# Expert weights of a mixture-of-experts encoder: gate and up loads cut in half along the contraction, down loads of the third pair moved up

## What is computed

```python
for g in range(N_GROUPS):
    a = jnp.einsum('td,edf->tef', t, w_gate[g])      # d = 1024, f = 256
    u = jnp.einsum('td,edf->tef', t, w_up[g])
    act = jax.nn.silu(a) * u * combine[:, g, :, None]
    y = y + jnp.einsum('tef,efd->td', act, w_down[g])
```

## Time and profile before

| | |
|---|---|
| time of the profiled execution | 859.02 us |
| its span | 857.3 us |
| median of three runs | 860.95 us |
| PE busy | 781.7 us (91% of the span) |
| DVE, ACT, POOL busy | 378.9, 282.9, 143.8 us |
| gate and up products (L1869) | 226.3 us busy, 25% of the chain that ended last |
| down products (L1895) | 122.4 us busy, 14% of the chain |
| moved by DMA | 245.52 MB, 286 GB/s over the span |

### The profile page before, as it was taken

How to read it: one execution, slowest core, us unless ns; L and a number is a source line. 1 busy time by engine, 2 the same in 40 slices (tenths; PEclk the granted TensorE clock), 3 DMA queues, 4 the chain that set the end, 5 groups by cost and what they waited for, 6 DMA issues and landing times.

```text
span 857.3 us, 11051 instructions
## 1 busy us (share of the span) xinstructions
PE 781.7 (91%) x4303; PEld 426.8 (50%) x4303; DVE 378.9 (44%) x701; ACT 282.9 (33%) x522; POOL 143.8 (17%) x135
## 2 busy tenths in 40 slices
PE   3877889999999999899999878998999999989897
PEld 3656835534434333346888655455343434434355
DVE  6998543622122221217858678426212222121164
ACT  5251143522121221216755445324212122121163
POOL 6695500200000000000066563001000000000000
PEclk9988989999999999999999889999999999999999
DMA  6052195399999999996579550352699999999931
GB/s 222 1 156 100 23 425 232 119 373 420 420 421 421 421 421 421 421 404 234 196 177 314 223 169 1 159 234 99 277 421 421 420 421 421 421 420 422 410 126 49
DMA packets 55493, 245.52 MB, mean 286 GB/s; under 512 B 14002, under 2 KB 15088, under 8 KB 30480
## 3 DMA queue, kind: packets, MB, share of 16 engines
q1 hardware_dynamic: 53344, 240.34, 70.1%
q0 software_dynamic: 2096, 4.45, 2.6%
HBM read 243.17 MB, written 1.60 MB: 286 GB/s over the span
## 4 chain that ended last, share of the span: by engine, by line
PE 80%; DVE 8%; POOL 4%; issue 4%; ACT 2%; DMA 1%; SPq 0%; DVEq 0%; ACTq 0%
PE PS L1869 25%; PE PS L1895 14%; PE PS L1646 11%; PE PS L1909 7%; PE PS L1805 3%; PE PS L2143 3%; PE PS L2118 2%; PE PS L1760 2%; PE PS L1820 2%; PE PS L2097 2%; PE PS L2029 2%; POOL s5V L608 2%; PE PS L1739 1%; POOL qrs L677 1%; PE PS L1878 1%
## 5 line engine op out<-in xcount | busy, mean ns | idle before, releaser
L1869 PE MATMUL PS<-ring,xw 128*64 128x512 f32 x1024 | 226.3, 593 | 14.1 <-issue 12.5
L1869 PEld LDWEIGHTS PS<-ring,xw 128*64 128x64 f32 x1024 | 77.3, 137 | 155.8 <-issue 155.7
L1895 PE MATMUL PS<-ring,actT 128*64 128x512 f32 x512 | 122.4, 603 | 1.4 <-DVE actT L1373 1.4
L572 POOL TENSOR_TENSOR rstd<-ms,mhalf 128x2 f32<-128x2 f32 x6 | 4.3, 710 | 583.6 <-DVE ms L1037 578.2
L1373 DVE COPY actT<-PS 128x256 f32<-128x256 f32 x32 | 13.6, 424 | 179.6 <-PE PS L1878 172.0
L886 ACT ACTIVATE ohi<-PS 128x512 fp32r<-128x512 f32 x64 | 38.2, 598 | 160.6 <-PE PS L1895 160.6
L1062 DVE SCALAR_TENSOR_TENSOR ringr<-ring,gcol,dwh 128x512 fp32r<-128x512 f32 x80 | 62.8, 835 | 26.9 <-ACT dwh L737 26.9
L1387 DVE TENSOR_TENSOR olo<-PS,ohi 128x512 fp32r<-128x512 f32 x64 | 44.1, 689 | 63.8 <-ACT ohi L886 62.3
L878 ACT ACTIVATE act<-PS,wslot 128x256 f32<-128x256 f32 x32 | 15.2, 474 | 171.7 <-PE PS L1869 171.7
L737 ACT ACTIVATE dwh<-ring,gcol 128x512 fp32r<-128x512 f32 x80 | 52.8, 716 | 34.2 <-PE PS L1646 34.2
L1646 PE MATMUL PS<-ringr,hTh 128*128 128x512 f32 x160 | 63.2, 395 | 0.0
(11 more groups left out here) (332 smaller groups left out, 1060.8 us busy)
## 6 DMA issues: line engine op xcount, KB each, us to landing
ring<-in_moe_w_gate SPq DMA_DIRECT2D x64, 1024.0 KB
ring<-in_moe_w_up SPq DMA_DIRECT2D x64, 1024.0 KB
ring<-in_moe_w_down SPq DMA_DIRECT2D x64, 1024.0 KB, 25.6
ring<-in_nat_w_qkv SPq DMA_DIRECT2D x6, 2048.0 KB
ring<-in_ple_w_gate SPq DMA_DIRECT2D x4, 2048.0 KB
ring<-in_s_w_out SPq DMA_DIRECT2D x2, 2048.0 KB
ring<-in_nat_w_o SPq DMA_DIRECT2D x2, 2048.0 KB
ring<-in_s_w_in SPq DMA_DIRECT2D x1, 2048.0 KB
```

Source lines behind the costliest of these rows:

```text
L1869: ins = mm(PS[CAP * h_:CAP * h_ + CAP, 0, :].rearrange("p (u f) -> p u f", u=2), xw[:, p % 2, k, CAP * h_:CAP * h_ + CAP], wv[h_][:, k], s ...
L1895: ins = mm(PS[CAP * h_:CAP * h_ + CAP, 2 + n, :], actT[:, k, CAP * h_:CAP * h_ + CAP], wd[h_][:, k, 512 * n:512 * n + 512], start=k == 0, ...
```

## The change

`load_gate_up` becomes two functions. `load_early` asks for floats 0 to 1023 of gate and of up (k = 0 to 3 of the contraction), after a new signal `gu_half`, which the last product of k = 3 of pair p - 3 gives. `load_late` asks for the other halves after `gu_done` as before. Each of the four loads of an expert is 0.5 MiB, 4 KB in one piece per partition. PE waits for the early halves at the start of `gate_up` and for the late ones ahead of k = 4, by a semaphore of their own for each two slots. The down loads of pair 2 are asked for right behind its gate and up loads, ahead of those of pair 3. To stay within the number of semaphores, some others are merged: the down loads of two slots share one; in the setup of the first layer `rp_loaded` and `gcol_loaded` become `vectors_loaded`, `dt_ready` goes into `trig_ready`, and `ldt_wide` into `ang_ready`.

```diff
@@ the waits @@
         loaded = [S(f"slot_loaded{s}") for s in range(6)]
-        down_loaded = [S(f"down_loaded{s}") for s in range(6)]
+        late_loaded = [S(f"late_loaded{s}") for s in range(3)]
+        down_loaded = [S(f"down_loaded{s}") for s in range(3)]
...
+        def late_arrived(eng, n):
+            eng.wait_ge(late_loaded[items[n][0] // 2], 64 * nth_moe[n])
+
         def down_arrived(eng, n):
-            eng.wait_ge(down_loaded[items[n][0]], 16 * nth_moe[n])
+            eng.wait_ge(down_loaded[items[n][0] // 2], 32 * nth_moe[n])
@@ SP @@
-            def load_gate_up(n):
+            def load_early(n):
+
+                s, (gate_, up_, _) = items[n]
+                if prev[n] is not None:
+                    name, value = done[prev[n]]
+                    sp.wait_ge(S("gu_half" if name == "gu_done" else name), value)
+                sp.dma_start(ring[s][:, 0:1024], gate_[1][:, 0:1024]).then_inc(loaded[s], 32)
+                sp.dma_start(ring[s][:, 2048:3072], up_[1][:, 0:1024]).then_inc(loaded[s], 16)
+
+            def load_late(n):
+
                 s, (gate_, up_, _) = items[n]
                 if prev[n] is not None:
                     name, value = done[prev[n]]
                     sp.wait_ge(S(name), value)
-                sp.dma_start(ring[s][:, 0:2048], gate_[1]).then_inc(loaded[s], 32)
-                sp.dma_start(ring[s][:, 2048:4096], up_[1]).then_inc(loaded[s], 16)
+                sp.dma_start(ring[s][:, 1024:2048], gate_[1][:, 1024:2048]).then_inc(late_loaded[s // 2], 16)
+                sp.dma_start(ring[s][:, 3072:4096], up_[1][:, 1024:2048]).then_inc(late_loaded[s // 2], 16)
...
-                        load_gate_up(m0 + 2 * p)
-                        load_gate_up(m0 + 2 * p + 1)
-
-                    if p < 2:
+                        load_early(m0 + 2 * p)
+                        load_early(m0 + 2 * p + 1)
+                        load_late(m0 + 2 * p)
+                        load_late(m0 + 2 * p + 1)
+
+                    if p < 3:
                         load_down(i, 2 * p)
                         load_down(i, 2 * p + 1)
-                    elif p > 2:
+                    elif p > 3:
@@ PE, gate_up and down @@
                 for k in range(k0, k1):
+                    if k == KD // 2:
+                        late_arrived(pe, moe_item[i] + 2 * p)
...
+                    if k == KD // 2 - 1:
+                        ins.then_inc(S("gu_half"), 1)
...
-                    if n == 0:
+                    if n == 0 and h_ == 0:
                         down_arrived(pe, it)
```

More of the change, by code:

```diff
@@ L451, in load_down @@
                     sp.wait_ge(S("d_done"), 2 * (NP * i + (e - 6) // 2) + 2)
-                sp.dma_start(ring[s][:, 4096:6144], down_[1]).then_inc(down_loaded[s], 16)
+                sp.dma_start(ring[s][:, 4096:6144], down_[1]).then_inc(down_loaded[s // 2], 16)
             sp.dma_start(lam[:, 0], I["s5_lam_re"][0].rearrange("d g p -> g d p")).then_inc(S("lam_loaded"), 16)
@@ L630, in _ @@
                 pool.dma_start(gcol[:, BLOCK_GAIN[n], :], gains[n].rearrange("(k p) -> p k", p=P),
-                               allow_slow_non_contiguous=True).then_inc(S("gcol_loaded"), 16)
+                               allow_slow_non_contiguous=True).then_inc(S("vectors_loaded"), 16)
             for n in (1, 4):
                 pool.dma_start(gcol[:, ROW_GAIN[n], :], gains[n].rearrange("(p k) -> p k", p=P))\
-                    .then_inc(S("gcol_loaded"), 16)
+                    .then_inc(S("vectors_loaded"), 16)
             pool.dma_start(rp[:, :, :], I["nat_rpb"][0].rearrange("a b c -> (a b) c")
                            .rearrange("(p a) c -> p a c", a=2))\
-                .then_inc(S("rp_loaded"), 16)
-            pool.wait_ge(S("rp_loaded"), 16)
+                .then_inc(S("vectors_loaded"), 16)
+            pool.wait_ge(S("vectors_loaded"), 16 * 8)
             link(pool.tensor_copy(rpf[:, :, :], rp[:, :, ::-1]))
@@ L641, in _ @@
             pool.wait_ge(S("rpbr_written"), 16)
-            pool.wait_ge(S("gcol_loaded"), 16 * 7)
+            pool.wait_ge(S("vectors_loaded"), 16 * 8)
             router_gain(0)
@@ L750, in _ @@
             ac.activation(dtt[:, :].rearrange("p (b j) -> p b j", j=4), perm(PS[:, 5, 0:SG]), ACT.Exp)\
-                .then_inc(S("dt_ready"), 1)
-            ac.wait_ge(S("ang_ready"), 1)
+                .then_inc(S("trig_ready"), 1)
+            ac.wait_ge(S("ang_ready"), 2)
             ac.activation(pq[:, 6], pq[:, 3], ACT.Sin).then_inc(S("trig_ready"), 1)
@@ L837, in _ @@
                 front(1, n)
-            ac.wait_ge(S("gcol_loaded"), 16 * 7)
+            ac.wait_ge(S("vectors_loaded"), 16 * 8)
             def gather_evict(i, k):
@@ L1073, in _ @@
             ve.wait_ge(S("lam_loaded"), 48)
-            ve.tensor_copy(ldtb[:, :, :], bc(ldt[:, :], 2, SP_)).then_inc(S("ldt_wide"), 1)
+            ve.tensor_copy(ldtb[:, :, :], bc(ldt[:, :], 2, SP_)).then_inc(S("ang_ready"), 1)
             ve.wait_ge(S("prm_T"), 1)
@@ L1079, in _ @@
                                 PS[:, 4, 0:2 * SG].rearrange("p (c j b) -> p c b j", c=2, j=4)))
-            ve.wait_ge(S("dt_ready"), 1)
+            ve.wait_ge(S("trig_ready"), 1)
             link(tt(v[1], im, dtt[:, :], ALU.mult))
@@ L1112, in _ @@
                     .then_inc(S("h_ready"), 1)
-            ve.wait_ge(S("trig_ready"), 3)
+            ve.wait_ge(S("trig_ready"), 4)
             link(tt(v[8], v[5], v[7], ALU.mult))
@@ L1654, in _ @@
                 pe.transpose(PS[:, 4, SG * c:SG * c + SG], lam[:, c].rearrange("g d p -> g (d p)"), ident[0:SG, 0:SG])
-            pe.wait_ge(S("ldt_wide"), 1)
+            pe.wait_ge(S("ang_ready"), 1)
             pe.transpose(PS[:, 5, 0:SG], ldtb[:, :, :].rearrange("g d p -> g (d p)"), ident[0:SG, 0:SG]).then_inc(S("prm_T"), 1)
```

## The result

The changed kernel took 853.43 us (median of six runs, 851.67 to 857.26), the kernel before beside it 861.02 (857.71 to 862.39): a ratio of 0.9924, with an interval of 0.9895 to 0.9954. It is faster, by 7.6 us (the difference of the medians) where the sum had 14.7, and lies above the range of 842.5 to 852.5. The profiled execution took 855.27 us, its span 853.5.

What follows compares the result with a forecast made beforehand. PE waits for weights late in both expert stages; starting the loads earlier wins 7.4 us in layer 0 and 7.3 in layer 1, 14.7 in all, from a mean of 859.7 to 845.0 us, range 842.5 to 852.5.

Steps and rivals of the forecast that it cites:

- the sum: Whole kernel: 7.4 us won in layer 0 and 7.3 in layer 1, 14.7 us in all.
- What bounds the kernel: Expert stages of both layers: PE waits for weights near the end, its lead used up by pair 12.
- the forecast 7.4 and 7.3: Gains in layers 0 and 1: waits of 6.3 and 6.2 us, plus 1.1 each for slower groups.
- The 358.0 for pair 15 without waits: Layer 0: start of pair 15 if PE never waited, in place of 365.31.
- Down loads moved: Pair 2's down loads run in the idle stretch of each layer; the stream behind is 5.0 us shorter.
- The early start: Pair 3 in each layer: `gu_half` comes 4.7 us ahead of `gu_done`, so the stream starts 4.7 us earlier.
- Rate of the shorter pieces: Gate and up loads: 4 KB pieces taken at 421 GB/s; down to 403 PE's work hides the price.
- the 5.8 us to spare: Pair 15, layer 0: late halves come at 355.6 and are needed at 361.4.
- My check of that load: Input of `p_transposes` behind pair 15: PE forward by 7.4 us, stream by 9.7, so it stays covered.
- Added wait, more loads, merges: Wait ahead of k = 4, ten issues for six a pair, merged signals: nothing; the wait at most 6.6 us.
- Everything behind is released by PE's progress and moves along: Work after the expert stages: moves forward with PE, keeping the gains of 7.4 and 7.3 us.
- part of it is lost: Rival: added wait costs up to 0.22 us each, or halves run at 403 to 384 GB/s; 848 to 856, chance 0.14.

Runs made afterwards that it cites:

- e4: The change with halves for pair 3 alone, all other pairs' gate and up in whole loads after `gu_done`, down loads moved: 849.15 us, 0.9881 of the kernel before.
- e5: The change with the early halves too asked for only after `gu_done`, so no early start: 861.04 us, 1.0011 of the kernel before.
- e2: The kernel before with pair 2's down loads moved and the setup's signals merged, gate and up in whole loads after `gu_done`: 854.8 us, ratio 0.9948.

## Why the prediction was wrong

*What bounds the kernel*: right. With weights in time, pairs take 6.87 us and steps 13.1 to 13.4, in both layers, and e4 shows that nearly the whole wait could be won: 6.9 and 6.7 us of the forecast 7.4 and 7.3. (The 358.0 for pair 15 without waits should have been 358.1, which changes nothing.)

*Down loads moved*: right. Alone, they brought pair 15 forward by the 5.0 us forecast, with 2.2 us of waiting left. The stage was shorter by 3.3 only, because the clock fell behind that wait.

*The early start*: the stream did start earlier, and `gu_half` was worth 3.1 to 4.0 us a layer (change against e5). But "its four loads of 0.52 MB last 5.0 us" assumed full rate at once. At 283 GB/s for 174 to 180, the stream falls short of 412 by 6 x 129 = 0.77 MB, 1.9 us.

*Rate of the shorter pieces*: **the step that failed**, together with the full rate at once, just above. The prediction put the price of the pieces at nothing. I took 421 GB/s from two single microseconds of `w_out`. The full stretch runs at 412 with a third of the bytes still in 8 KB pieces: 6.29 MB / 0.412 = 15.27 us a pair, less 4.98 for the down loads, leaves 10.29 us for 4.19 MB, or 408 GB/s. The figure that I had set beside the row, the 408.7 GB/s of the Trainium skill (DMA: Bandwidth & Descriptors, section "iDMA fabric — 4 AXI ports for 8 engines, asymmetric across TPBs"), was the right one; the trace agrees with it. Over 13 pairs it costs 13 x 0.33 = 4.3 us. With the slow start, 6.2 of the 5.8 us to spare are gone: PE waits 0.5 us for pair 15's late halves. And the lead that is left, 9.7 - 4.3 - 1.9 = 3.5 us, is 3.4 short of the 6.9 by which PE is forward after that wait: the load for `p_transposes`, 2.3 us early before, should be 1.1 late, and PE waited 1.7 in layer 0 and 1.1 in layer 1. My check of that load had used the lead without its losses. The rate alone would have left both covered, by 1.5 and 0.3 us; it took the slow start too, for which the prediction had no term. These waits, 2.2 and 1.9 us a layer, are most of the 2.6 and 2.3 that the stages lack to 7.4 and 7.3.

*Added wait, more loads, merges*: nothing, as taken. Groups take 6.87 with the wait in their middle.

*"Everything behind is released by PE's progress and moves along"*: wrong by 2.2 to 2.5 us in the profiled executions. The second mixer, in which the clock falls, took longer behind the changed stage. Its cause is open.

*The sum* for the profiled executions: 4.75 + 4.97 won, 2.5 lost in the middle, and 3.4 lost ahead of the first stage, where the changed kernel's profiled execution was late (167.60) and its second one was not (164.32). Of the 7.1 us that the medians lack to the 14.7, the stages explain 5.0 and the middle about 2. The rival "part of it is lost" came true in its time (848 to 856), but not by either of its conditions: the added wait cost nothing, and the rate was 408, not 403 to 384. That was too strict, because 408 used up what I called spare once the start was slow. I gave that case 0.14.

## What to carry to other kernels

Before cutting loads in pieces, ask where the queue is empty: only there can a load start sooner. Cut those loads and leave the rest whole (e4), and first look for loads that stand behind a wait which isn't theirs, as moving them cost nothing here. A margin that hides a price must be worked out with every loss at once, for each consumer on the way; and a rate is read from a long stretch, not from single microseconds. What is left of a wait can cost more than its length when the clock falls behind it, as in e2. Where TensorE's clock falls between two stages, that stretch may change its length too, so compare stage by stage.

## What the hardware showed

A stream with gate and up in 4 KB pieces and down in 8 KB pieces runs at 412 to 413 GB/s, against 421 with all in 8 KB pieces, whatever the size of a load (0.5 or 1 MiB). That makes 408 for the 4 KB pieces, if the others keep 421.

After a pause such a stream runs at 200 to 350 GB/s in most of its first 7 or 8 microseconds, with the engines' share about 1. With 8 KB pieces it doesn't (e2 has 431 GB/s at 174 to 180). Why is open, and the length of the pieces alone doesn't explain it: the load of `w_out` in the kernel before, 4 KB pieces behind a pause as well, reaches 365 and 422 GB/s within 4 us of its first bytes:

```profile
73.00:74.00 1.00, 0.00 (x0) 0.00 (x0) 0.97 (x2) 0.00 (x0) 1.00 (x1) 1.00 0.98 365
74.00:75.00 1.00, 0.80 (x7) 0.83 (x9) 0.84 (x6) 0.00 (x0) 0.08 (x1) 0.61 1.02 422
```

A stream with two thirds of its bytes in loads to 64 partitions ran at 227 GB/s. A wait of 2.2 us ahead of a group was followed by half clock in e2, one of 2.0 in the kernel before was not. The expert stages repeat to within 0.1 us in the kernel before and 0.9 in the changed one, while whole executions of one kernel differ by up to 11 us.
